# The first mixing stage of a transformer kernel begins by row tile, with its first four projection units in two pairs

## What is computed

```python
f = _swiglu(_rmsnorm(x, ffn1_pre_g[l]), ffn1_w_gate[l], ffn1_w_up[l], ffn1_w_down[l])
x = x + 0.5 * _rmsnorm(f, ffn1_post_g[l])

h = _rmsnorm(x, mix_pre_g[l])
qkv = h @ w_qkv[l]
qa, ka, va, qb, kb, vb = jnp.split(qkv, QKV_SPLITS, axis=-1)
qa = _apply_axial_rope(_rmsnorm(qa, q_norm_g[l]), ang_row, ang_col)   # ka alike
out_a = _gqa_dense_blocked(qa, ka, va)
qb, kb = _apply_rope(qb, ang_1d), _apply_rope(kb, ang_1d)
out_b = _dilated_mixture(qb, kb, vb)
x = x + _rmsnorm(concatenate([out_a, out_b]) @ w_out[l], mix_post_g[l])
```

## Time and profile before

| | |
|---|---|
| median of 3 runs | 1088.11 us (1087.91 to 1088.23) |
| the profiled execution | 1087.55 us, of which the profile's span is 1085.7 |
| TensorE busy | 99% of the span |
| VectorE, ScalarE, GpSimd busy | 73%, 54%, 20% |
| first FFN's last matmul group ends | 195.47 us |
| first mixing stage, TensorE | 195.47 to 303.7 us |

### The profile page before, as it was taken

One profiled execution on the slowest core, in us unless ns is written; L12 is line 12 of the kernel. 1 busy time (PEld: TensorE's weight loads), 2 busy tenths in 40 slices (PEclk: granted clock), 3 DMA queues, 4 the chain that ended last, 5 costly groups with the idle time before them and its releaser, 6 DMA issues.

```text
span 1085.7 us, 18945 instructions
## 1 busy us (share of the span) xinstructions
PE 1069.9 (99%) x7134; PEld 945.8 (87%) x7134; DVE 789.5 (73%) x1083; ACT 587.8 (54%) x839; POOL 216.1 (20%) x223
## 2 busy tenths in 40 slices
PE   8999999999999999999999999999999999999997
PEld 8888889898788888898998988888899889888886
DVE  5867776886678888766775788777558557777674
ACT  6546444667666545455785644454443565544452
POOL 0006000031069997000000398000000000000000
PEclk9999999999999999999999999999999999999999
DMA  7765445342345646453334655654434235545541
GB/s 258 291 247 204 174 179 207 111 162 78 120 158 193 233 181 232 174 192 119 126 147 155 228 199 189 220 189 174 174 120 158 97 134 180 226 174 179 206 155 40
DMA packets 36514, 189.65 MB, mean 175 GB/s; under 512 B 3824, under 2 KB 4592, under 8 KB 21616
## 3 DMA queue, kind: packets, MB, share of 16 engines
q1 hardware_dynamic: 34016, 181.22, 46.3%
q10 hardware_dynamic: 2160, 6.70, 1.8%
q0 software_dynamic: 288, 1.05, 0.3%
HBM read 187.90 MB, written 1.05 MB: 174 GB/s over the span
## 4 chain that ended last, share of the span: by engine, by line
PE 89%; DVE 6%; ACT 3%; issue 1%; DMA 1%; DVEq 0%; SPq 0%; ACTq 0%
PE ps L529 23%; PE ps L600 19%; PE ps L534 12%; PE ps L639 10%; PE ps L741 6%; PE ps L541 6%; PE ps L561 2%; PE ps L661 1%; DVE gu_low L1687 1%; PE ps L576 1%; PE ps L490 1%; PE ps L588 1%; PE ps L694 1%; PE ps L725 1%; PE ps L707 1%
## 5 line engine op out<-in xcount | busy, mean ns | idle before, releaser
L529 PE MATMUL ps<-hT,gu_high 128*128 128x512 f32 x1152 | 286.8, 391 | 0.0
L529 PEld LDWEIGHTS ps<-hT,gu_high 128*128 128x128 f32 x1152 | 211.5, 188 | 41.6 <-issue 0.4
L1814 DVE TENSOR_TENSOR gu_low<-gu_raw,gu_high 128x2048 fp32r<-128x2048 f32 x83 | 195.9, 2361 | 7.4 <-ACT gu_high L1208 4.4
L534 PEld LDWEIGHTS ps<-hT,gu_low 128*128 128x128 f32 x1152 | 157.2, 190 | 11.2
L1208 ACT ACTIVATE gu_high<-gu_raw 128x2048 fp32r<-128x2048 f32 x84 | 160.4, 1910 | 9.3 <-PE ps L541 8.3
L534 PE MATMUL ps<-hT,gu_low 128*128 128x256 f32 x1152 | 160.6, 282 | 0.0
L1184 ACT ACTIVATE ffn_s<-ffn_s 128x256 f32<-128x256 f32 x88 | 36.8, 418 | 180.1 <-DVE ffn_s L1781 144.0
L1818 DVE TENSOR_TENSOR dn_low<-dn_raw,dn_high 128x1024 fp32r<-128x1024 f32 x84 | 112.2, 1336 | 2.7 <-ACT dn_high L1216 2.7
L1796 DVE TENSOR_TENSOR ffn_s<-ps,ffn_s 128x256 f32<-128x256 f32 x72 | 30.6, 425 | 109.1 <-ACT ffn_s L1196 109.1
L1687 DVE TENSOR_TENSOR gu_low<-gu_raw,gu_high 128x2048 fp32r<-128x2048 f32 x36 | 83.4, 2316 | 34.6 <-ACT gu_high L1102 34.6
L1216 ACT ACTIVATE dn_high<-dn_raw 128x1024 fp32r<-128x1024 f32 x84 | 88.7, 1056 | 35.8 <-PE ps L600 35.8
(11 more groups left out here) (327 smaller groups left out, 1873.0 us busy)
## 6 DMA issues: line engine op xcount, KB each, us to landing
gu_raw<-in_wgu SPq DMA_DIRECT2D x126, 1024.0 KB, 4.8
dn_raw<-in_wdn SPq DMA_DIRECT2D x88, 512.0 KB, 5.2
x<-in_x SPq DMA_DIRECT2D x2, 512.0 KB, 5.6
gu_raw<-in_wgu SPq DMA_DIRECT2D x2, 512.0 KB, 6.8
scratch<-in_glu ACTq DMA_DIRECT2D x1, 1024.0 KB, 7.9
scratch<-in_biasM ACTq DMA_DIRECT2D x1, 1024.0 KB, 5.4
s5in<-in_s5in ACTq DMA_DIRECT2D x1, 768.0 KB, 4.3
out_x<-scratch SPq DMA_DIRECT2D x3, 256.0 KB, 2.4
```

What stands on the lines that cost most here:

```text
L529: nc.tensor.matmul(out, gu[0][:, sl, o:o + P], hT_both[:, k, :, :].rearrange("p a s -> p (a s)"), start=k == 0, stop=False)
L534: i = nc.tensor.matmul(out[:, 0:SEQ], gu[1][:, sl, o:o + P], hT[0][:, k, :], start=False, stop=k == KC - 1)
L1814: nc.vector.tensor_tensor(gu[1][:, sl, :], gu_raw[:, sl, :], gu[0][:, sl, :], ALU.subtract).then_inc(s["gu_split"], 1)
```

## The change

The first mixing stage now begins with tile 0 alone. After the FFN, ScalarE takes the square sum of each bank (`post_ffn_square`), VectorE puts both halves of tile 0 into x first (`after_first_ffn`), TensorE transposes tile 0 whole, and ScalarE and VectorE evict 128x128 pieces (`tile_out`, `tile_low`). TensorE then multiplies tile 0 by the first pair of units while tile 1 is finished and transposed in between.

Units 0 to 3 are made as two pairs (`pair_unit`). A pair is 48 matmuls with a moving operand of 512 columns, 256 of each unit: 24 for tile 0 into one bank, 24 for tile 1 into the next. An item of a pair holds four chunks of both units, loaded from two stored items at once. The items of pair 0 are stored items 0 and 2, those of pair 1 items 1 and 3. The item that opens pair 1 is split in two halves (`pair_high_half`).

Orders: TensorE makes `rope_transposes(0)` inside pair 1, unit 4, `rope_transposes(1)`, `pair_scores(0)`, unit 5, `rope_transposes(2)`, `pair_scores(1)`. On VectorE each split that stood between rope steps is one item later (item 3 where item 2 was), `pair_max(0)` stands before `rope_sum(2)`, the reciprocals of constants go behind `rope_turn(1)`, and from `rope_turn(4)` on nothing is moved. ScalarE has `pair_exps(0)` before `rope_raw(4)` and unit 5's values before `rope_in_out(2)`. Semaphore counts are adapted. The diff, cut:

```diff
-ORDER0 = (2, 0, 1, 3, 5, 7, 4, 6, 8)
+ORDER0 = (None, None, None, None, 5, 7, 4, 6, 8)
 ORDER1 = (0, 1, 4, 6, 5, 7, 2, 3, 8, 9)
 ORDER2 = (0, 1, 2, 4, 6, 3, 5, 7)
 HEADS = 4
...
-            order = (0, 1, 2, 3) if p in (1, 6) else (0, 2, 1, 3)
+            order = (0, 1, 2, 3) if p in (0, 1, 6) else (0, 2, 1, 3)
             engine.wait_ge(s["x_ready"], 4 * p + order.index(k) + 1)
         def unit_bank(pos):
...
+            return bank(2 + 4 * pair + t)
+        def tile_chunk(t, c):
+            return (bank(4 + c) if c < 4 else bank(c % 2)[:, c // 2 % 2 * P:])[:, 0:P]
+        def by_pair(buffer, slot):
+            return buffer[:, slot, :].rearrange("p (u n) -> p u n", u=2)
         def wait_unit(engine, m, j):
-            if m == 0 and j in ROPE_AT:
...
+                engine.wait_ge(s["raw_ready"], 2)
+            elif m == 0 and j in ROPE_AT:
                 engine.wait_ge(s["raw_ready"], ROPE_AT.index(j) + 1)
             elif m == 0:
                 engine.wait_ge(s["proj_free"], 1 if j == 5 else 2)
...
                     sp_.wait_ge(s["gu_split"], g - 1)
+                if isinstance(g, int) and 0 <= g - MIX_ITEM[0] < 4:
+                    u, c = MIX_ITEM[0] + (g - MIX_ITEM[0]) // 2, (g - MIX_ITEM[0]) % 2 * 1024
+                    sp_.dma_start(by_pair(gu_raw, slot),
+                                  a["wgu"][u:u + 3:2, :, c:c + 1024].rearrange("u p n -> p u n")) \
+                       .then_inc(gu_loaded[slot], 16)
+                    return
                 for m in range(3):
                     first_out = MIX_ITEM[m] + MIX_IN[m]
                     if isinstance(g, int) and first_out <= g < first_out + MIX_OUT:
...
                 pe.wait_ge(s["gu_split"], item + 1)
-                if v >= 2:
+                if (m, v) in ((0, 4), (0, 5)):
+                    wait_unit(pe, 0, "pair 0")
+                elif v >= 2:
                     wait_unit(pe, m, 0 if v < 4 else v - 2)
                 for h in halves:
                     for k in range(KC):
...
+            def pair_unit(pair, q, t, ks, ready=None):
+                item = MIX_ITEM[0] + 2 * pair + q
+                for k in ks:
+                    if pair == 1 and t == 0 and q == 0 and k % 4 in (0, 2):
+                        pe.wait_ge(*((s["pair_half"], 1) if k == 0 else (s["gu_split"], item + 1)))
+                    elif k % 4 == 0:
+                        pe.wait_ge(s["gu_split"], item + 1)
+                    if ready is not None:
+                        pe.wait_ge(*ready(k))
+                    for pw_, px in PASSES:
+                        both = gu[pw_][:, item % 2, :].rearrange("p (u k n) -> p k u n", u=2, k=4)[:, k % 4]
+                        i = nc.tensor.matmul(pair_of(pair, t).rearrange("p (u n) -> p u n", u=2),
+                                             hT[px][:, k, t * P:(t + 1) * P], both,
+                                             start=(pw_, px, k) == (0, 0, 0), stop=(pw_, px, k) == (1, 0, KC - 1))
+                if t == 1:
+                    i.then_inc(s["proj_done"], 1)
+                elif ks[-1] == KC - 1:
+                    i.then_inc(s["pair_t0"], 1)
             def rest_of_x(n):
...
             ffn(0, 0, lambda: rest_of_x(0))
-            fill(5, 7)
+            def chunk_of(t):
+                return lambda k: (s["tile_low"], KC * t + k + 1)
+            fill(3, 7)
             transposes(1, 0, 0)
-            fill(3, 7)
+            transposes(1, 0, 1)
+            pe.wait_ge(s["gained"], 3)
+            pair_unit(0, 0, 0, range(4), chunk_of(0))
+            pair_unit(0, 1, 0, range(4, 5), chunk_of(0))
             transposes(1, 1, 0)
-            project_first(0, 1, False, lambda: rest_of_x(1))
-            for v in range(1, 3):
-                project(0, v, False)
-            for k in range(3):
-                rope_transposes(k)
-                if k < 2:
-                    project(0, 3 + k, False)
+            pair_unit(0, 1, 0, range(5, 7), chunk_of(0))
+            pe.wait_ge(s["tile_low"], KC)
+            transposes(1, 1, 1)
+            pair_unit(0, 1, 0, range(7, 8), chunk_of(0))
+            for q in range(2):
+                pair_unit(0, q, 1, range(4 * q, 4 * q + 4), chunk_of(1))
+            pair_unit(1, 0, 0, range(4))
+            pair_unit(1, 0, 1, range(4))
+            pair_unit(1, 1, 0, range(4, 8))
+            rope_transposes(0)
+            pair_unit(1, 1, 1, range(4, 8))
+            project(0, 4, False)
+            rope_transposes(1)
             pair_scores(0)
             project(0, 5, False)
+            rope_transposes(2)
             pair_scores(1)
             rope_transposes(3)
             pair_transposes(0)
...
                   .then_inc(s["half_high" if w == 0 else "gu_high"], 1)
+            def pair_high_half(w):
+                g = MIX_ITEM[0] + 2
+                wait_used(act, g - 2)
+                act.wait_ge(gu_loaded[g % 2], loaded(g))
+                ks = slice(w * 512, w * 512 + 512)
+                nc.scalar.activation(by_pair(gu[0], g % 2)[:, :, ks], by_pair(gu_raw, g % 2)[:, :, ks], ACT.Copy) \
+                  .then_inc(s["half_high" if w == 0 else "gu_high"], 1)
             def dn_high_first(f):
                 act.wait_ge(dn_loaded[0], loaded(FCH * f))
...
                 act.dma_start(a["out"][:, 0, 512:], postw[:, 0, 512:]).then_inc(s["out_stored"], 16)
+            def tile_out(n, t):
+                ts_ = slice(t * P, (t + 1) * P)
+                for c in range(KC):
+                    act.wait_ge(s["tile_psum"], KC * t + (c + 1 if c < 4 else KC))
+                    if c >= 6:
+                        act.wait_ge(s["tile_low"], KC * t + c - 1)
+                    nc.scalar.activation(hT[0][:, c, ts_], tile_chunk(t, c), ACT.Copy,
+                                         scale=col(COL_GAIN + n * KC + c)).then_inc(s["tile_high"], 1)
             def norm_out(n, chunks=range(KC)):
...
+            def post_ffn_square(k):
+                t = k // 2
+                wait_bank(act, 0, k)
+                if k == 1:
+                    act.wait_ge(s["gained"], 1)
+                nc.scalar.activation(squares[:, k, :], bank(k), ACT.Square, scale=st["rinv"][:, t:t + 1],
+                                     accum_out=st["pss"][:, k:k + 1]).then_inc(s["psq_done"], 1)
+                if k % 2:
+                    act.wait_ge(s["psq_done"], k + 1)
+                    act.wait_ge(s["post_mean"], t + 1)
+                    nc.scalar.activation(st["pstd"][:, t:t + 1], st["pss"][:, k:k + 1], ACT.Sqrt, scale=4.0 / D,
+                                         bias=st["pmean0"][:, t:t + 1]).then_inc(s["pstd_ready"], 1)
             def post_ffn(p):
...
-            norm_out(1, range(4))
-            norm(1, (0,))
-            norm_out(1, range(4, KC))
-            norm(1, (1,))
+            for k in range(2 * TT):
+                post_ffn_square(k)
+            for t in range(TT):
+                tile_out(1, t)
+                norm(1, (t,))
             def rope_in_out(k):
...
+            def pair_raw(k, t):
+                pair, r = k // 2, ROPES[k]
+                act.wait_ge(*((s["pair_t0"], pair + 1) if t == 0 else (s["proj_done"], 2 * pair + 2)))
+                if k >= 2:
+                    act.wait_ge(s["rop_ready"], k - 1)
+                if k == 0:
+                    act.wait_ge(s["rinv_ready"], 3 + t)
+                w = rope_heads(r) * HD
+                src = pair_of(pair, t)[:, SEQ * (r in (2, 3)):]
+                if r == 2:
+                    nc.scalar.activation(vA[:, t, :], src[:, P:2 * P], ACT.Copy, scale=st["rinv"][:, t:t + 1])
+                i = nc.scalar.activation(raw[:, k % 2, t * w:(t + 1) * w], src[:, 0:w], ACT.Copy,
+                                         scale=st["rinv"][:, t:t + 1])
+                if t == 1:
+                    i.then_inc(s["raw_ready"], 1)
             def rope_std(k):
...
-            for k in range(3):
-                rope_raw(k)
-                next_high(k)
-                if k == 2:
-                    rope_in_out(0)
-                rope_std(k)
+            for w in range(2):
+                pair_high_half(w)
+            for t in range(TT):
+                for k in range(2):
+                    pair_raw(k, t)
+            next_high(1)
+            rope_std(0)
+            next_high(2)
+            rope_std(1)
+            pair_raw(2, 0)
+            rope_in_out(0)
+            pair_raw(2, 1)
+            next_high(3)
+            for t in range(TT):
+                pair_raw(3, t)
+            rope_std(2)
             step.mark(nc.scalar.activation(st["warm"][:, 0:1], col(COL_HALFPI), ACT.Exp))
             step.done(act)
-            rope_raw(3)
-            next_high(3)
             rope_in_out(1)
+            next_high(4)
+            pair_exps(0)
             rope_raw(4)
-            next_high(4)
+            values_in(5)
             rope_in_out(2)
-            pair_exps(0)
-            values_in(5)
             next_high(5)
```

(67 more changed lines are left out.)

49 lines of the change are left out of this document (25 added, 24 removed).

## The result

The changed kernel takes 1090.44 us (median of 10 runs, 1089.82 to 1091.71), the kernel before beside it 1087.87 us (10 runs). The ratio of the two is 1.0027, with an interval from 1.0019 to 1.0035: it is slower, by 0.27%. The prediction was 1088.6 us with a range up to 1091.4; the time lies inside, and where rival B had put it (1090.5). The profiled execution took 1091.45 us, with a span of 1089.7.

A forecast was written before the change was run, and what follows sets the result against it. TensorE was taken as full, VectorE nearly full up to 240 us. TensorE's -2.6 and the +3.1 wait give +0.5: 1087.55 + 0.5 + 0.56 = 1088.6 us, own range 1087.5 to 1089.8, with rivals 1085.7 to 1091.4.

The forecast's parts named there:

- rival B: The clock falls in TensorE's 3.1 us wait before `pair_transposes(0)`: 1.9 us more, 1090.5 us; chance 0.27.
- The entry: From the first FFN to the first projection matmul, which starts at about 197.8, 2.1 us sooner.
- the pairs: Units 0 to 3 on TensorE: 96 matmuls of 512 columns for 192 of 256, 1.1 us saved.
- unit 4: TensorE reaches unit 4, behind the pairs, at 221.7 instead of 225.59, 3.9 us ahead.
- The new wait before `pair_scores(0)`: TensorE waits 0.8 us for `rope_in_out(1)` on ScalarE, so the scores start at 228.85.
- The wait before `pair_transposes(0)`: TensorE, ready at 237.9, waits 3.1 us for VectorE's `pair_normal(0)` and starts at 241.0, 0.5 later than before.
- item 4's load: Weight load starting at 210.75, landing in 4.8 us; at 6.1 us it would be late by 0.2.
- the 0.6 us that the prediction gives to GpSimd beside VectorE: In VectorE's queue before `pair_normal(0)`: GpSimd working beside VectorE decides 0.6 us of the later start.
- the replay: VectorE's queue reckoned instruction by instruction up to `pair_normal(0)`, ending at 240.95; the method allowed 0.5 us either way.
- The end moves with it, us for us: From `pair_transposes(0)` to the output units stays 37.9 us, without waits, so a later start moves the end equally.
- Rival A: TensorE's 2.6 us gain arrives, VectorE's gaps (1.2 and 1.4 us) not being work: 1086.0 us; chance 0.2.
- Rival C: Entry or splits not as reckoned, or loads late by over 1 us: 1 to 2 us later, 1090; chance 0.05.

The follow-up runs named there:

- e0_after: The changed kernel again, unaltered: 1090.36 us, 2.8 us above the kernel before.
- e8_fill5: The changed kernel with 10 dummy matmuls on TensorE ahead of `pair_transposes(0)`: 1089.39 us, 1.9 us above the kernel before.
- after: The changed kernel itself, in its first measurement beside the kernel before: 1090.44 us.
- e5_fill13: The changed kernel with 26 dummy matmuls on TensorE ahead of `pair_transposes(0)`: 1090.12 us, 2.6 us above the kernel before.
- e2_recip: The changed kernel with VectorE's `constant_reciprocals()` (1.75 us) moved from ahead of `pair_normal(0)` to behind `pair_low(0)`: 1090.14 us.
- e6_best: The changed kernel with VectorE's `pair_normal(0)` behind turn 3, `pair_max(1)` before turn 4, sum 4 behind `pair_max(2)`; TensorE's `pair_transposes(0)` before `rope_transposes(3)`: 1085.84 us.
- e11_best_again: e6_best run again, unaltered: 1085.85 us, 1.6 us below the kernel before.

## Why the prediction was right or wrong

**The entry, the pairs, unit 4: right.** The first 512-column matmul starts at 197.84 (197.8 predicted). Unit 4 starts at 221.37 (221.7). The pairs' matmuls come 0.2275 us apart: from the timeline of the changed kernel,

```profile
211.84 0.62 PE L710 MATMUL ps<-gu_high,hT 128*128 128x512 f32 x2
212.29 0.39 PE L710 MATMUL ps<-gu_low,hT 128*128 128x512 f32 x1
212.52 0.62 PE L710 MATMUL ps<-gu_high,hT 128*128 128x512 f32 x2
```

three in 0.68 us. 96 of them are 21.8 us, and 192 of the earlier trace rows are 23.0: 1.2 us saved, where 1.1 stood in the sum. One of 512 columns cost 0.2275 us, and the two of 256 that it replaces cost 0.240: 12.5 ns apart, where the prediction read 11 from the rows. VectorE's 128x128 pieces came 0.26 us apart (four from 197.34 to 198.39), for 0.27 taken.

**The new wait before `pair_scores(0)`: right.** 228.91 after 1.18 us (228.85 after 0.8), released by `rope_in_out(1)`.

**The wait before `pair_transposes(0)`: right in kind, short by 0.5 us and more.** Predicted was a start at 241.0 after 3.1 us, 0.5 later than before; it was 241.47 after 3.34, and 0.98 later than before when both are counted from the fillers (46.02 against 45.04), 1.43 in e0_after. The largest term that was mis-sized is item 4's load. The prediction took 4.8 us for it, and said that at 6.1 it would be late by 0.2. The rows of the changed kernel, the load issued at 210.7 and the next one:

```profile
DMA to landing us min/median/max: 6.1/6.1/6.1
...
DMA to landing us min/median/max: 4.8/4.8/4.8
```

In the eleven traces of kernels with the change this load took 6.0 to 6.7 us, about at the upper bound or above it, and the next one 4.7 to 5.1. VectorE's idle time ahead of that split was 0.52 us at a landing of 6.0 (e8_fill5), 0.54 at 6.1 (after), 1.00 at 6.5 (e0_after), 1.16 at 6.7 (e5_fill13), and `pair_transposes(0)` came 46.01, 46.02, 46.47 and 46.65 us behind the fillers. Between these four traces 0.7 us of landing go with 0.64 of start; no run changed the load alone. Taken back from 46.0 by the 0.52 us that the split waited, this gives 45.5, which is the prediction's +0.5.

That this comes out so well is partly luck. VectorE was ready for the split at 218.28, 0.27 sooner than reckoned, waited 0.54 and began it at 218.82. From there to `pair_max(0)` it took 11.33 us for 11.45 reckoned, and from `pair_max(0)` at 230.15 to the end of `pair_normal(0)` at 241.42 it took 11.27 for 10.95. Those 10.95 are not what the prediction prints either: its terms from 230.0 on add up to 10.6, and 240.6. Two of the three rope sums cost 0.79 to the next start where 0.6 stood, and `pair_max(0)` 1.47 where 1.35 stood. No run tests the 0.6 us that the prediction gives to GpSimd beside VectorE; the trace shows 0.55, the split beside GpSimd at 2.83 us and one without it at 2.28. So the replay had the path right, with misses of 0.1 to 0.7 us in its parts that in part cancelled.

**Behind `pair_transposes(0)`: right where the clock stayed.** 37.93 us to the output units in the kernel before, 37.97 in e0_after, 37.98 in e5_fill13, with no new waits. "The end moves with it, us for us" held.

**The clock: taken for the less likely case, and it was the likely one.** Rival B had 0.27. All of its signs came in the first trace: the wait of 3 us, the fall 2.2 us into it (2.1 was read from the earlier trace rows), a clock below 1.00 from 240 on, which the prediction had named as a sign of its being wrong. Its price was put at 1.9 us within 3.8; it is 86.57 - 46.02 - 37.97 = 2.6 us in the changed kernel's trace, 1.5 in those of e2_recip and e8_fill5 (85.72 - 46.24 - 37.97, 85.49 - 46.01 - 37.97), and 0 in e0_after. The step that failed is the weighing: with a forecast wait of 3.1 us and a fall that the trace of before shows about 2.1 us into idleness, the clock's fall belonged in the forecast, and its chance should have been over a half: of the 21 executions of the changed kernel 18 have a mean clock of 0.996 or 0.997, of the 87 of the kernel before in the experiments' rounds three. The sum would then have been 1087.55 + 0.56 + 0.5 + 1.9 = 1090.5, and the measured median is 1090.44; that this agrees to a tenth is partly luck, since `pair_transposes(0)` came 0.5 us later than reckoned, the clock's price differs from execution to execution (0, 1.5 and 2.6 us in three traces), and it does not always fall. The same holds for the forecast as it stood: 1090.44 lies 1.8 us above 1088.6 and outside its own range (1087.5 to 1089.8), and only the room made for the rivals takes it in. The traces give the clock as a share of full speed, and only 1.00 and 0.50 occur in them, where the prediction says 2.4 and 1.2 GHz: at 0.50 256 columns took 0.213 us, 1.2 columns per ns, and at 1.00 512 columns took 0.1075 us more than 256, 2.4 columns per ns for those added.

**Rival A** (TensorE's gain arrives) needed VectorE's gaps to close by themselves. They don't, but e6_best shows that they can be closed: with its order the stage is 1.5 us shorter than before, of the 2.6 forecast (2.1 us in e11_best_again). **Rival C** (splits or loads late by over 1 us) did not come in the changed kernel's first trace, though its mechanism, a late load, was present at half its size (0.54 us of waiting for the split); in five other traces with the change that wait was 1.0 to 1.2 us.

What the fit of the parts does not settle: the median of e5_fill13 stands 1 us above what its stage accounts for. Its trace has the excess in the opening of the kernel and behind the stage, and why it comes in half of the executions stays open. That the opening alone can cost 2 us is seen in the trace of e11_best_again (below).

## What to carry to other kernels

Shortening the work of a full engine ahead of a stretch where a second engine is nearly full buys only as much as the second engine's order lets through; so change the order of the second engine with it, and look for what TensorE needs standing behind a handover to a third engine. Work that stands in such a handover costs little: taking it out gained 0.2 us of 1.75 (e2_recip). If a forecast leaves TensorE waiting for over 2 us, count the loss of the clock behind it in the forecast itself: in these traces it fell at five of eight such waits, for 3.4 or 6.8 us, and in the mixing stage a fall cost 1.5 us (e2_recip, e8_fill5) or 2.6 (the changed kernel). And compare edits of 1 us by the length of the stage in the trace, from a common event in front to a common event behind, not by single executions of the whole.
